# Moving the weight slots of two stages by 192 bytes in SBUF

## What is computed

```
mod = silu(c) @ ada_w + ada_b                      # per layer
h = rms_norm(x, norm_mix_g) * (1 + sc_m) + sh_m
proj = h @ w_in                                    # 1952 columns for attention, 3 x 1024 for gates
merged = sum over branches of gate_n * (o_n @ w_br_n)
x = x + g_m * (merged @ w_out)
h = rms_norm(x, norm_ffn_g) * (1 + sc_f) + sh_f
x = x + g_f * ((silu(h @ gate) * (h @ up)) @ ffn_w_down)
...
proj = x @ w_in_2 ; four recurrences/attentions y_n
merged = sum_n sigmoid(merge_n) * (y_n @ w_branch_2[n]) ; h = merged @ w_out_2
moe: 2 experts of 16 for each token, of width 512
```

## The kernel before

| buffer | start modulo 256, before | after | used with |
|---|---|---|---|
| hT_pair (normed tokens) | 128 | 128 | all three rings |
| layer_split, layer_raw | 64 | 0 | layers |
| merge_pair | 128 | 128 | layer_split, 256 columns |
| ffnh_aT | 64 | 0 | layer_split, 512 columns |
| split_w, raw_w | 64 | 0 | mixer |
| mixer_pair | 64 | 0 | split_w, 512 columns |
| expert_split, gathered_pair, gather_table | 128 | 128 | experts |
| x3_pair | 0 | 0 | stationary, with gather_table moving |
| the attention's buffers (branch_gates, o_tok, proj_tok, na_qkT) | 64 | 0 | small matmuls, most with constants at 128 |
| mixer_arena | 160 | 96 | small matmuls of the recurrences |

## Time and profile before

### The profile page before, as it was taken

One profiled execution on the slowest core, in us unless ns is written; L12 is line 12 of the kernel. 1 busy time (PEld: TensorE's weight loads), 2 busy tenths in 40 slices (PEclk: granted clock), 3 DMA queues, 4 the chain that ended last, 5 costly groups with the idle time before them and its releaser, 6 DMA issues. The chain is left out here.

```text
span 1783.0 us, 25495 instructions
## 1 busy us (share of the span) xinstructions
PE 1584.5 (89%) x10701; PEld 1435.6 (81%) x10701; DVE 1224.1 (69%) x1352; ACT 818.9 (46%) x952; POOL 43.5 (2%) x60
## 2 busy tenths in 40 slices
PE   2799997999989999899969999787688979999995
PEld 2789987999888988799959898686677777888884
DVE  4877577888756648666545784633565868899895
ACT  1345543443334553434323465224453346777774
POOL 0100000000010000000000000000000000000000
PEclk9999999999989999999989999897897988999998
DMA  8974435999854324566536563111231546999993
GB/s 306 316 241 139 162 128 160 353 334 321 282 149 142 118 96 144 199 207 218 167 87 189 157 190 119 53 42 48 71 95 48 186 147 238 376 362 371 360 363 124
DMA packets 226055, 348.04 MB, mean 195 GB/s; under 512 B 14612, under 2 KB 156672, under 8 KB 225808
## 3 DMA queue, kind: packets, MB, share of 16 engines
q1 hardware_dynamic: 225936, 346.36, 58.2%
HBM read 345.29 MB, written 1.97 MB: 195 GB/s over the span
## 5 line engine op out<-in xcount | busy, mean ns | idle before, releaser
L459 PE MATMUL bank<-layer_split,hT_pair 128*128 128x256 f32 (+2 forms) x4032 | 512.9, 287 | 30.7 <-DVE hT_pair L1033 21.4
L459 PEld LDWEIGHTS bank<-layer_split,hT_pair 128*128 128x128 f32 x4032 | 486.6, 191 | 44.6 <-issue 29.3
L184 DVE TENSOR_TENSOR layer_split<-layer_raw,layer_split 128x2048 fp32r<-128x2048 f32 x122 | 279.6, 2292 | 100.5 <-ACT layer_split L172 98.9
L172 ACT ACTIVATE layer_split<-layer_raw 128x2048 fp32r<-128x2048 f32 x122 | 233.6, 1915 | 190.3 <-PE bank L459 73.0
L184 DVE TENSOR_TENSOR expert_split<-expert_raw,expert_split 128x2048 fp32r<-128x2048 f32 x96 | 219.0, 2289 | 26.4 <-ACT expert_split L172 25.9
L172 ACT ACTIVATE expert_split<-expert_raw 128x2048 fp32r<-128x2048 f32 x96 | 183.4, 1917 | 55.7 <-PE bank L2470 31.4
L459 PE MATMUL bank<-split_w,hT_pair 128*128 128x256 f32 (+1 forms) x1248 | 169.3, 297 | 13.7 <-PEq L2704 5.0
L459 PEld LDWEIGHTS bank<-split_w,hT_pair 128*128 128x128 f32 x1248 | 159.2, 196 | 24.1 <-issue 16.2
L184 DVE TENSOR_TENSOR split_w<-raw_w,split_w 128x2048 fp32r<-128x2048 f32 x52 | 119.2, 2292 | 63.6 <-ACT split_w L172 63.0
L1896 PE MATMUL bank<-layer_split,ffnh_aT 128*128 128x512 f32 x528 | 127.0, 396 | 2.8 <-DVE ffnh_aT L1964 2.8
L172 ACT ACTIVATE split_w<-raw_w 128x2048 fp32r<-128x2048 f32 x52 | 99.4, 1912 | 58.1 <-PE bank L459 49.7
(11 more groups left out here) (466 smaller groups left out, 1888.4 us busy)
## 6 DMA issues: line engine op xcount, KB each, us to landing
layer_raw<-in_ada_w SPq DMA_DIRECT2D x48, 1024.0 KB, 6.5
layer_raw<-in_ffn_w_gate_up SPq DMA_DIRECT2D x44, 1024.0 KB, 5.7
raw_w<-in_w_in SPq DMA_DIRECT2D x40, 1024.0 KB, 5.3
layer_raw<-in_w_in SPq DMA_DIRECT2D x38, 1024.0 KB, 6.4
expert_raw<-in_w_gate SPq DMA_DIRECT2D x32, 1024.0 KB, 7.2
expert_raw<-in_w_up SPq DMA_DIRECT2D x32, 1024.0 KB, 7.6
expert_raw<-in_w_down SPq DMA_DIRECT2D x32, 1024.0 KB, 7.3
layer_raw<-in_ffn_w_down SPq DMA_DIRECT2D x22, 1024.0 KB, 5.7
```

The costliest lines, as they stand in the source:

```text
L172: self.nc.scalar.activation(self.pair[:, j % self.pairs, 0, 0:self.size[n]], self.raw[:, n % self.depth, 0:self.size[n]], ACT.Copy).then_i ...
L184: self.nc.vector.tensor_tensor(self.pair[:, j % self.pairs, 1, 0:self.size[n]], self.raw[:, n % self.depth, 0:self.size[n]], self.pair[:, ...
L459: ins = nc.tensor.matmul(out, lhs, rhs, start=first and c == chunks[0] and tp + wp == 0, stop=last and c == chunks[-1] and tp == 1)
```

## The change

```diff
@@ layers()
                 acc0, acc1 = sb("ada_acc", [P, D], st), sb("ada_acc_1", [P, D], st)
+                sb("offset_layer_ring", [P, 48], st)
                 ring = Ring(nc, "layer", sb("layer_raw", [P, 4, UNIT], st), sb("layer_split", [P, 3, 2, UNIT], st, FR), units,
@@ LayerBuffers
-                sb("offset_merge_pair", [P, 16], st)
+                sb("offset_merge_pair", [P, 32], st)
                 self.pair = sb("merge_pair", [P, 2, 2, 4, S], st, FR)
-                sb("offset_ffnh_aT", [P, 48], st)
+                sb("offset_ffnh_aT", [P, 32], st)
                 self.aT = sb("ffnh_aT", [P, 2, 2, S], st, FR)
@@ second_part()
             with ExitStack() as st:
+                sb("offset_mixer_ring", [P, 48], st)
                 ring = Ring(nc, "second", sb("raw_w", [P, 3, UNIT], st), sb("split_w", [P, 2, 2, UNIT], st, FR), units)
```

## The result

The changed kernel takes 1811.73 us (median of 4 runs, 1804.42 to 1812.56) beside 1791.57 us for the kernel before: a ratio of 1.0107, with a 95% interval of 1.0089 to 1.0125. It is slower by 19 us by this ratio, by 20 us from median to median. Its profiled execution has a span of 1810.9 us against 1783.0.

The account below looks back on a forecast made before the run. PE's distance between matmul starts was taken as the bound outside the recurrences. Gains of 4.1 + 2.8 + 0.4 + 0.6 = 7.9 us, counted as 7.5, gave 1792.9 - 7.5 = 1785.4 us; range 1781 to 1806, 8 times in 10.

Parts of the forecast that it names:

- What bounds the kernel: Whole kernel outside the recurrences: PE is busy 89% of the span, so the distance between matmul starts sets the time.
- Two paces that a stream keeps: PE streams of 256 columns: a fast or a slow pace, 4.5 ns apart for each matmul, kept once taken.
- the fast bound: All moved matmul streams: at distance 128 all keep the fast pace, as no row shows a faster one.
- fm -4.1 us: 256-column products with tokens moving, weights stationary: 955 of 1152 now in slow streams turn fast, saving 4.1 us.
- tok -3.2: 256-column products with tokens stationary: 627 slow ones turn fast, 2.8 us, plus 0.4 us beside the recurrences.
- 512 columns -0.6: 288 products of 512 columns in 12 blocks: the experts' pace would save 1.2 us, half of it counted, 0.6 us.
- the slow pace spreading: Rival: fast tokens-stationary products turn slow at 128, 4483 costing 20.2 us; 1797 to 1812 us, chance 0.23.
- Nothing moves: Rival: the moment a stream starts sets its pace, not the distance; 1792.9 us, between 1789.5 and 1796, chance 0.23.
- a rule: Skill's statement on TensorE's read ports, set against the forecast: operand addresses can't matter, the time would stay.
- DVE: Splitting units on DVE: offset worth nothing between 64 and 128; at offset 0 bounded by 3 ns each, 0.5 us.
- The clock: Rival: one more half-clock stretch of PE would cost about 5 us; chance 0.02, shared with dearer small matmuls.

Follow-up runs that it names:

- the two profiles: Against the kernel before, weight units of tokens-moving products and of 512-column branch products written at their own offsets, run twice: 1787.50 us (1.0001) and 1790.20 us (0.9999).

## Why the prediction was wrong

- **What bounds the kernel** was right: DVE, ACT and DMA did not enter into it, and 23.7 us more between PE's starts became 19 us of time.
- **Two paces that a stream keeps** was right for distances 192 and 64, with the 4.5 ns between them. Other distances have paces of their own.
- **The failed step** is the fast bound taken as the forecast: "all of them keep the fast pace, as no row shows a faster one". It took distance 128 to be at least as good as 192 with no row at 128, from two findings that don't bear on it: 512 columns are fast at 0, and some streams at 192 are slow. The runs show 113.3 at 192 for nearly all streams and at 64 for some, and at 128 only 118.7 or 120.0; at 0 it is 120.0. Each of the three terms of the sum was built on it: fm -4.1 us came out at +1.7, tok -3.2 at +20.3 with merge_pair at +1.8 beside it, 512 columns -0.6 at -0.2 (the distances between starts of the two traces).
- **The error beneath it** was the missing sign. The tables gave fm and tok jobs the same distance, 192, so that fm slow and tok fast looked like chance or a matter of role, which a better distance might cure for both. With moving less stationary, the rows of before already fit one function, but for single streams: 192 fast for 256 columns, 64 slow, 0 fast and 192 slow for 512. Then 128 would have been an unknown point beside the best known one for 5280 of the 6432 products of 256 columns, and a loss the likelier outcome.
- **The rival that came true** is the slow pace spreading: all tok products over, fm unchanged, 1812.6 us. The measured median is 1811.7. Its mechanism and place were right, as was the remark that the feed-forwards had nothing to win and all to lose. Its price was near: it took the slow pace to be 117.8 at the new distance too, 20.2 us for 4483 products, where 118.7 and 120.0 made it 22.1 us between starts, of which not all reached the time. That the time came within 1 us of it is in part luck. Its chance of 0.23 was too small, and the range left out its upper half, which is where the time fell.
- **"Nothing moves"** was wrong, and with it what the prediction drew from a rule. The Trainium skill, "SBUF — State Buffer", section "Who interferes with whom", calls TensorE's two read ports independent and says that PE never waits on anyone. The measurement speaks against taking this as a rule for time: with no other engine at work, the same stream takes 113.3 or 120.0 ns for each matmul by the difference of its operands' starts.
- **DVE** was right: its split costs 2292 ns at offset 0 as at 64.
- **The clock** was named as a rival for which the rows gave no reason, with about twice 113 ns for a matmul at half clock; measured are 213.3. In the profiled execution of after, 193 us are at half clock against 172 of before, which is part of why its span grew by 27.9 us where the medians differ by 20.

## What to carry to other kernels

Give moving and stationary operands of fp32r streams a signed distance, moving less stationary modulo 256 bytes, and tabulate it for each kind of product before an offset is touched: 192 was best for 256 columns and 0 for 512, and what was best for one was among the worst for the other. Two good points say nothing of a third: 128 was slow for both widths, and 8 bytes off 192 cost the whole gain. Ask such a question first of a kernel of bare streams, which answered in one run of 0.6 ms what this change got wrong.

## What the runs showed of the hardware

- The pace of a stream of fp32r matmuls depends on the difference of its operands' starts modulo 256 bytes, at full clock: for 256 columns 113.3 ns at 192, 117.8 and now and then 113.3 at 64, and 116.7 to 121.8 elsewhere, 8 bytes off 192 included; for 512 columns 226.7 ns at 0 and 228.9 to 234.3 elsewhere. It didn't depend on either start alone where that was tried (tokens at 128 and at 0), nor on which operand is which beyond the sign.
- At half clock (granted 0.50) the pace of 256 columns is 213.3 ns at distances 0, 64, 128 and 192 alike: what the distance costs is there at full clock only.
- At one distance more than one pace can be stable. Which one a stream takes is decided in its first few matmuls, and it keeps it for as long as it runs unbroken, over 340 matmuls in the longest. After a gap, one start 0.22 to 0.61 us behind the last, the same stream went on at the other pace in some cases.
- The mechanism behind the function of the distance was not found. Nothing here shows why 192 and 0 are the good ones, or why at the mirror distance, 64, the feed-forwards took the fast pace more often than streams alone.
- A gain between starts of 4.9 and 3.9 us in the two profiles left the time where it was, both times with 3.3 us more of the span's clock missing in the mean of the runs. Whether faster streams bring this about is open.
